# Gathers and scatters of a mixture-of-experts layer with 128 rows instead of 96

## What is computed

```python
scores = sigmoid(h @ w_router)
_, top_idx = top_k(scores + router_bias, 8)
top_w = top_s / sum(top_s) * 2.5
hmid = silu(h @ w_gate_e) * (h @ w_up_e) * gate     # each expert: 1024 -> 256
out = x + shared(h) + sum over chosen experts of hmid @ w_down_e   # 256 -> 1024
```

## Time and profile before

| | |
|---|---|
| median of 3 runs | 1163.53 us (1160.26 to 1170.39) |
| the profiled execution's own time | 1162.66 us |
| its span, first to last instruction | 1160.7 us |
| TensorE matmuls | busy 1116.2 us, 96% |
| VectorE | busy 875.0 us, 75% |
| ScalarE | busy 718.3 us, 62% |
| GpSimd | busy 337.8 us, 29% |
| DMA over the span | 284.64 MB, 245 GB/s; 16 engines |

### The profile page before, as it was taken

One profiled execution on the slowest core, in us unless ns is written; L12 is line 12 of the kernel. 1 busy time (PEld: TensorE's weight loads), 2 busy tenths in 40 slices (PEclk: granted clock), 3 DMA queues, 4 the chain that ended last, 5 costly groups with the idle time before them and its releaser, 6 DMA issues.

```text
span 1160.7 us, 18736 instructions
## 1 busy us (share of the span) xinstructions
PE 1116.2 (96%) x5682; PEld 828.7 (71%) x5682; DVE 875.0 (75%) x1445; ACT 718.3 (62%) x1218; POOL 337.8 (29%) x293
## 2 busy tenths in 40 slices
PE   7999999999999999999999999999999999999994
PEld 5889978777775575567777777777677767777772
DVE  6543385578753534589999999999899888999982
ACT  5434455453435111258888888888787877878882
POOL 0221021000000001136333344444444443455542
PEclk7999999999999999999999999999999999999997
DMA  5333221422422175459999999999999999999962
GB/s 182 129 90 117 85 72 39 152 66 82 119 82 82 64 322 203 170 209 381 370 365 366 373 370 369 368 360 368 367 368 368 354 353 356 368 364 365 363 193 32
DMA packets 65606, 284.64 MB, mean 245 GB/s; under 512 B 12515, under 2 KB 15083, under 8 KB 40604
## 3 DMA queue, kind: packets, MB, share of 16 engines
q1 hardware_dynamic: 51228, 250.50, 57.6%
q0 software_dynamic: 14336, 33.59, 12.2%
HBM read 271.40 MB, written 29.42 MB: 259 GB/s over the span
## 4 chain that ended last, share of the span: by engine, by line
DMA 47%; POOL 3%; issue 3%; POOLq 1%; DVE 0%
DMA out<-arena,idxs 47%; POOL turn L561 3%; POOLq L328 0%; POOL out L571 0%; POOLq L577 0%; POOLq L597 0%; POOLq L581 0%; DVE w_lo L1286 0%; POOLq L582 0%
## 5 line engine op out<-in xcount | busy, mean ns | idle before, releaser
L1657 PE MATMUL bank<-gu_parts,xT_parts 128*96 128x512 f32 x1280 | 343.6, 398 | 4.5 <-DVE xT_parts L1274 3.6
L1657 PEld LDWEIGHTS bank<-gu_parts,xT_parts 128*96 128x96 f32 x1280 | 202.0, 162 | 88.2 <-DVE xT_parts L1274 4.1
L561 POOL TENSOR_TENSOR turn<-minus_half 16x1 f32<-16x1 f32 x128 | 149.9, 1171 | 367.6 <-DMA out<-arena,idxs 319.4
L1672 PE MATMUL bank<-w_lo 128*96 128x512 f32 (+1 forms) x816 | 204.9, 400 | 3.9 <-issue 2.9
L1672 PEld LDWEIGHTS bank<-w_lo 128*96 128x96 f32 (+1 forms) x816 | 130.7, 167 | 51.1 <-issue 4.3
L1281 DVE TENSOR_TENSOR gu_parts<-arena_x,gu_parts 128x1024 fp32r<-128x1024 f32 x96 | 116.7, 1216 | 18.9 <-ACT gu_parts L862 18.9
L1488 PE MATMUL bank<-w_hi,hT_hi 128*128 128x512 f32 (+1 forms) x320 | 125.8, 393 | 3.7 <-DVE arena L1232 2.2
L1281 DVE TENSOR_TENSOR gu_parts<-arena,gu_parts 128x1024 fp32r<-128x1024 f32 x96 | 116.8, 1216 | 14.6 <-ACT gu_parts L862 14.6
L862 ACT ACTIVATE gu_parts<-arena_x 128x1024 fp32r<-128x1024 f32 x96 | 101.4, 1056 | 40.2 <-DMA arena_x<-in_w_up_e 28.8
L1488 PE MATMUL bank<-w_hi,hT_lo 128*128 128x512 f32 (+1 forms) x320 | 122.7, 383 | 0.0
L1488 PE MATMUL bank<-w_lo,hT_hi 128*128 128x512 f32 (+1 forms) x320 | 122.4, 383 | 0.0
(11 more groups left out here) (190 smaller groups left out, 1929.8 us busy)
## 6 DMA issues: line engine op xcount, KB each, us to landing
arena<-in_w_gate_e SPq DMA_DIRECT2D x32, 1024.0 KB
arena<-in_w_up_e SPq DMA_DIRECT2D x32, 1024.0 KB
arena<-in_w_down_e SPq DMA_DIRECT2D x32, 1024.0 KB
arena_x<-in_w_gate_e SPq DMA_DIRECT2D x32, 1024.0 KB
arena_x<-in_w_up_e SPq DMA_DIRECT2D x32, 1024.0 KB
arena_x<-in_w_down_e SPq DMA_DIRECT2D x32, 1024.0 KB
arena<-in_w_in SPq DMA_DIRECT2D x14, 1024.0 KB, 5.4
arena<-in_w_gate SPq DMA_DIRECT2D x8, 1024.0 KB, 5.8
```

The source lines that it names most:

```text
L561: nc.gpsimd.tensor_tensor(turn[:], minus_half[0:16, 0:1], minus_half[0:16, 0:1], ALU.add).then_inc(turns, 1)
L1657: last = nc.tensor.matmul(out_, a[:, PER * c + j, :], b[c][:, :, j, :], start=(c == 0 and j == 0 and i == 0), stop=(c == CHUNKS - 1 and j ...
L1672: last = nc.tensor.matmul(psY[h][0:rows, :], midT[n][a][:, j, 0:rows], w[b][:, j, h * 512:(h + 1) * 512], start=(j == 0 and k == 0), stop= ...
```

## The change

Both kinds of transfer take all 128 rows. `iota_b` is filled for 16 runs of eight partitions, slot m * 16 + i in partition 8 i + m, and `held` cuts the first six of each eight out of a tile: only these columns of the one-hot tile are ever written, the others stay zero from one memset, and their index is out of bounds. There are 96 slots as before. The weights of TensorE for the gathered rows, for `mid` and for the slots have 128 columns in place of 96, and the outputs 128 rows; the copies on ScalarE and VectorE of transposed data handle the same 96 columns as before in 16 runs of six, those that work by rows handle 128 partitions.

```diff
-        xT_hi, xT_lo = (xT_parts[:, k * ND * SLOTS:(k + 1) * ND * SLOTS].rearrange("p (j s) -> p j s", j=ND) for k in range(2))
+        xT_hi, xT_lo = (xT_parts[:, k * ND * P:(k + 1) * ND * P].rearrange("p (j s) -> p j s", j=ND) for k in range(2))
...
+        def held(t):
+            return t.rearrange("p j (i m) -> p j i m", i=DMA_ENGINES)[:, :, :, 0:SLOTS // DMA_ENGINES]
...
         def turned_rows(c):
-            return psT[c][:].rearrange("p (j s) -> p j s", j=HALF)[:, :, 0:SLOTS]
+            return psT[c][:].rearrange("p (j s) -> p j s", j=HALF)
+        def these_rows(k):
+            return (lambda t: t) if isinstance(k, int) and k == 0 else held
...
-                pool.indirect_dma_start(out=xg[slot][0:SLOTS, :], out_offset=None, in_=hn_dram,
-                                        in_offset=bass.IndirectOffsetOnAxis(idxg[slot][0:SLOTS, 0:1], 0),
+                pool.indirect_dma_start(out=xg[slot], out_offset=None, in_=hn_dram,
+                                        in_offset=bass.IndirectOffsetOnAxis(idxg[slot][:, 0:1], 0),
...
-                pool.indirect_dma_start(out=out_rows, out_offset=bass.IndirectOffsetOnAxis(idx[0:SLOTS, 0:1], 0),
-                                        in_=y[slot][0:SLOTS, :], in_offset=None, bounds_check=last_row, oob_is_err=False,
+                pool.indirect_dma_start(out=out_rows, out_offset=bass.IndirectOffsetOnAxis(idx[:, 0:1], 0),
+                                        in_=y[slot], in_offset=None, bounds_check=last_row, oob_is_err=False,
...
-                    nc.scalar.activation(xT_hi[:, c * HALF:(c + 1) * HALF, :], turned_rows(c), ACT.Copy).then_inc(xT_hi_ready, 1)
+                    nc.scalar.activation(these_rows(k)(xT_hi[:, c * HALF:(c + 1) * HALF, :]), these_rows(k)(turned_rows(c)), ACT.Copy).then_inc(xT_hi_ready, 1)
...
+            for n in range(2):
+                nc.vector.memset(onehot[n], 0.0)
...
-                return nc.vector.tensor_tensor(onehot[n][:, :, 0:SLOTS], iota_b[:, 0:SLOTS].unsqueeze(1).broadcast_to([P, NT, SLOTS]),
-                                               col.broadcast_to([P, NT, SLOTS]), ALU.is_equal)
+                to = held(onehot[n])
+                return nc.vector.tensor_tensor(to, held(iota_b[:].unsqueeze(1)).broadcast_to(to.shape), col.unsqueeze(3).broadcast_to(to.shape), ALU.is_equal)
...
-                    last = nc.tensor.matmul(psI[0:SLOTS, 0:6], onehot[n][:, t, 0:SLOTS], table[:, t, bass.ds(e, 1), :].rearrange("p a b -> p (a b)"),
+                    last = nc.tensor.matmul(psI[:, 0:6], onehot[n][:, t, :], table[:, t, bass.ds(e, 1), :].rearrange("p a b -> p (a b)"),
...
-                    last = nc.tensor.transpose(psT[j // HALF][:, c:c + SLOTS], xg[slot][0:SLOTS, j::ND], ident[0:SLOTS, 0:SLOTS])
+                    last = nc.tensor.transpose(psT[j // HALF][:, c:c + P], xg[slot][:, j::ND], ident)
...
-                    down(n, h, P if is_shared(it) else SLOTS).then_inc(y_psum, 1)
+                    down(n, h, P).then_inc(y_psum, 1)
...
-    c[:, P:P + SLOTS] = np.arange(SLOTS).reshape(SLOTS // DMA_ENGINES, DMA_ENGINES).T.reshape(-1)[None]
+    c[:, P:2 * P] = np.arange(P).reshape(P // DMA_ENGINES, DMA_ENGINES).T.reshape(-1)[None]
```

More of the change, by code:

```diff
@@ L820, in _, with silu_of, silu_i @@
             nc.scalar.activation(scoresT, psI[0:E, :], ACT.Sigmoid).then_inc(scores_sig, 1)
-            def silu_of(n, rows):
-                return nc.scalar.activation(silu[n][0:rows, :], psG[n][0:rows, 0:F], ACT.Silu)
+            def silu_of(n):
+                return nc.scalar.activation(silu[n], psG[n][:, 0:F], ACT.Silu)
             def copy_midT(n, rows):
-                return nc.scalar.activation(midT[n][0][:, :, 0:rows], psM[:, 0:NF * P].rearrange("p (j s) -> p j s", j=NF)[:, :, 0:rows], ACT.Copy)
+                these = held if rows == SLOTS else (lambda t: t)
+                return nc.scalar.activation(these(midT[n][0]), these(psM[:, 0:NF * P].rearrange("p (j s) -> p j s", j=NF)), ACT.Copy)
             def copy_y(n, h):
-                return nc.scalar.activation(y[n][0:SLOTS, h * 512:(h + 1) * 512], psY[h][0:SLOTS, :], ACT.Copy)
-            def silu_i(it, n, rows):
+                return nc.scalar.activation(y[n][:, h * 512:(h + 1) * 512], psY[h][:], ACT.Copy)
+            def silu_i(it, n):
                 act.wait_ge(gu_psum, it + 1)
                 after(act, mid_ready, it - 1)
-                silu_of(n, rows).then_inc(silu_ready, 1)
+                silu_of(n).then_inc(silu_ready, 1)
             def y_i(it, n):
@@ L905, in _ @@
                 gu_hi_k(1, 1, c)
-            silu_i(SH, 0, SLOTS)
+            silu_i(SH, 0)
             xT_hi_k(1)
@@ L1273, in xT_k @@
                     half = slice(c * HALF, (c + 1) * HALF)
-                    nc.vector.tensor_tensor(xT_lo[:, half, :], turned_rows(c), xT_hi[:, half, :].bitcast(f32), ALU.subtract).then_inc(xT_split, 1)
+                    nc.vector.tensor_tensor(these_rows(k)(xT_lo[:, half, :]), these_rows(k)(turned_rows(c)), these_rows(k)(xT_hi[:, half, :].bitcast(f32)), ALU.subtract).then_inc(xT_split, 1)
             def gu_lo_k(k, slot, c):
@@ L1283, in low_midT @@
             def low_midT(n, rows_):
-                src = psM[:, 0:NF * P].rearrange("p (j s) -> p j s", j=NF)[:, :, 0:rows_]
-                return nc.vector.tensor_tensor(midT[n][1][:, :, 0:rows_], src, midT[n][0][:, :, 0:rows_].bitcast(f32), ALU.subtract)
+                these = held if rows_ == SLOTS else (lambda t: t)
+                src = psM[:, 0:NF * P].rearrange("p (j s) -> p j s", j=NF)
+                return nc.vector.tensor_tensor(these(midT[n][1]), these(src), these(midT[n][0].bitcast(f32)), ALU.subtract)
             def low_wd(slot, h):
@@ L1709, in midT_i @@
                 after(pe, midT_ready, it)
-                transpose_mid(n, P if is_shared(it) else SLOTS).then_inc(midT_psum, 1)
+                transpose_mid(n, P).then_inc(midT_psum, 1)
             def find_i(it, n):
@@ L1785, in _ @@
                         pe.wait_ge(w_in_sem[0][k], 4 * E + 16 * it + 16)
-                    gate_up(0, SLOTS, xT_all, 0).then_inc(o_gu, 1)
+                    gate_up(0, P, xT_all, 0).then_inc(o_gu, 1)
                     pe.wait_ge(o_mid, it + 1)
-                    transpose_mid(0, SLOTS).then_inc(o_midT_psum, 1)
+                    transpose_mid(0, P).then_inc(o_midT_psum, 1)
                     pe.wait_ge(o_midT, it + 1)
                     pe.wait_ge(o_wd, it + 1)
-                    down(0, 0, SLOTS)
-                    down(0, 1, SLOTS).then_inc(o_y_psum, 1)
+                    down(0, 0, P)
+                    down(0, 1, P).then_inc(o_y_psum, 1)
                     pe.wait_ge(o_y, it + 1)
```

20 lines of the change are left out of this document (10 added, 10 removed).

## The result

The changed kernel takes 1227.24 us (median; 1225.65 to 1229.6), the kernel before beside it 1161.89 us: a ratio of 1.0551, 95% interval 1.0511 to 1.0590. That is 65.35 us slower. The direction was forecast, the size was three times too small, and the result lies 5 us above the range.

What follows compares the result with a forecast made beforehand. TensorE was taken to bound the early experts, weight loading the late ones, with the scatter chain equally long. Chain growth of +15.6 us early and +5.4 late gave +21 on the profiled 1162.66: 1184 us, range 1142 to 1222.

Steps and rivals of the forecast that it cites:

- The scatter chain: Experts: each scatter into `out` waits for the last to land; 9.60 us apart early, 10.37 late, as long as the period.
- The signs given for it: Experts: 18432 packets, same bytes, landing near 9.4 us, one regime about 10.3 us, scatter waits up, up-weight waits down.
- the rival of the half of the engines: Indirect transfers: half the engines get eight rows with data, the others almost none; about 1253 us, chance 0.18.
- the term for the scatter's landing: Scatter: empty rows 0.63 us and POOL's work 0.17, together 0.8 us for each scatter, between 0 and 1.1.
- eight rows for each engine, the same four with data, four empty: Indirect transfers of 128 rows: how rows were taken to fall on each engine, bytes unchanged, 144 packets.
- The 0.63 itself: Scatter: two more empty rows, each with a weight packet of 0.315 us, put the completion up to 0.63 us later.
- 0.65 and 0.15: Expert period: growth in us for each of the first 24 periods (+15.6 us) and the last 36 (+5.4 us).
- the aligned partitions give back nothing: Gather beside weight loads: less conflict was worth 0.5 to 0.7 us an expert, at most 24.5 us in all; taken as 0.
- the rival (0.6 us an expert in the late stretch, 1142 us): Gather and weights: the conflict goes and the chain has slack, late period 9.7 us; 1142 us, chance 0.18.
- The two ends that I let cancel: Aligned partitions: at most 24.5 us gained, at least below nothing as the same writes meet on fewer partitions; taken as 0.
- the wider instructions: TensorE, VectorE and ScalarE at 128 wide: under 0.1 us an expert on TensorE, set at nothing.
- POOL's own 0.17 us: POOL's work for each scatter of 128 rows: 0.17 us more, a third of the upper end 0.48.

Runs made afterwards that it cites:

- e1_quads: The changed kernel with slots laid out for a deal in fours, three of each four partitions in use; 1138.78 us.
- e5_scatter_96: The changed kernel with slots in sixes over the first 96 partitions, the gather kept at 128 rows, the scatter back at 96; 1142.56 us.
- e7_ports_worst: e2_96_wide with only the slot order inside each engine's six partitions changed, so rows crowd on fewer groups of four partitions; 1174.52 us.
- the square: Four kernels, slots in sixes, gather/scatter rows: 96/96 1162.8 us, 128/96 1142.56, 96/128 1188.44, 128/128 1193.78.
- e2_96_wide: The changed kernel with both transfers back at 96 rows filled by sixes, all other instructions still 128 wide; 1162.8 us.
- e3_112: e2_96_wide with transfers of 112 rows, seven partitions for each engine, six of them in use; 1154.0 us.

## Why the prediction was wrong

**Right: what bounds the kernel, and by which mechanism it would slow.** The scatter chain was named as long as the expert period and as what becomes the bound when it grows. The signs given for it came in kind: 18432 packets and unchanged bytes, ScalarE waiting for scatters (3.3 us before, 170.7 after), the up-weight waits nearly gone, one regime instead of two. Their sizes did not: the landing was to be 9.4 us before 750 us and was about 10.4, the period about 10.3 and was 11.15. The rate stayed under 340 GB/s all through (333 and 325), which was the sign named for the rival of the half of the engines.

**Wrong: the term for the scatter's landing.** The step that failed is "eight rows for each engine, the same four with data, four empty". The bytes were right and the deal was not: the fullest engine has 7.92 rows with data on average instead of 4.47. I priced two empty rows at 0.63 us beside a weight packet each. The time from a scatter's issue to the turn that it releases in fact grew by 1.7 us in the first stretch (8.8 to 10.4) and by 1.1 in the second (9.3 to 10.4). `e1_quads`, with the same 32 empty rows more, has 9.0 and 9.3 us there; so all but a few tenths are the deal. The rows with data alone grew by 2.2 us in their span (2.55 to 4.79, first stretch); from the last of them to the released turn it is then 0.8 us in place of 1.6, which gives some back, and why is not shown.

The 0.63 itself rested on a wrong reading of the earlier trace rows. Of the 24 packets under 512 B only 15 are of POOL's queue; the other 9 are of the weight queue, and 60 beside 71 does not tell whether a weight packet goes between two empty rows. After the change 64 empty rows pass in 0.24 us (807.72 to 807.96). By the deal in fours they are eight for each engine that has no data, and a weight packet before each would have made it 8 x 0.309 = 2.5 us.

The period of the experts became, by the scatters' spacing, 11.15 us: 1.55 more than 9.60 in the first stretch and 0.78 more than 10.37 in the second. With the forecast's 24 and 36 periods that is 37 + 28 = 65 us, as measured; with the SiLU's 9.62 and 10.30 us in their place it would be 67, so the agreement to the microsecond is chance. The forecast had 0.65 and 0.15.

**Wrong: the aligned partitions give back nothing.** The conflict did go, 432 GB/s against 317, and the price put on it in the rival (0.6 us an expert in the late stretch, 1142 us) is nearly what `e5_scatter_96` and `e1_quads` got, 1142.56 and 1138.78; their late period is 9.8 us by the SiLU (757.8 to 1080 us), where the rival had 9.7. The two ends that I let cancel did not: the thought that rows on fewer partitions would meet more weight writes did not hold for gathers of 128 rows, wherever their rows lay: in the six kernels that have them 5 to 7% of the weight packets took over 340 ns (527 to 1080 us), in the five whose gathers have 96 or 112 rows 18 to 26%. The reading that fits is that in a transfer of 128 rows the engine that writes a row is the one that loads the weights there; the traces do not name the engine of a packet, so it is argued and not shown. In the 96-row form crowding does cost: 11.7 us in `e7_ports_worst`. The statement that the gain would lie under the longer chain in any case was right for the changed kernel, and the square shows it: 20 us of gain under the short scatter, none under the long one.

**Right: the wider instructions.** Taken as nothing; 0.9998 (0.9971 to 1.0024) in `e2_96_wide`. POOL's own 0.17 us measured 0.147.

**The rivals.** "The rows with data fall on half of the engines" was the case, at a chance of 0.18 and 1253 us. Its price was too high, and its parts were wrong: it charged gathered and scattered rows alike, 2.2 us an expert, less 0.7. By the square the gather's extra rows are hidden beside the scatter chain; and it left out that a weight packet goes behind each row. 3.45 rows more at 0.327 + 0.309 us are 2.2, the growth of the scattered rows' span. Its own sum was not consistent either: 11.8 against a mean period of 10.0 is 1.8 and not 1.5, and 60 times that is 108 us.
The Trainium skill (DMA: Bandwidth & Descriptors, The descriptor swizzle) gives the deal of a plain transfer to 128 partitions: four and four, 32 apart. The runs agree, for transfers by index too: this rule is what `e1_quads` was built on, and it was 88 us faster than the deal in eights that the filling assumed. I gave it 0.18 because no row of before showed a 128-row transfer by index; a rule about the same number of partitions from the same queue deserved more than that.
The Trainium skill (SBUF — State Buffer, Door 1: The DMA port swizzle) has fours of partitions on ports, two fours that are 32 apart on each. `e7_ports_worst` was laid out by that rule and took 11.7 us more than `e2_96_wide`, so it agrees in direction; the size at one port was not measured.

**What stays open.** `e1_quads` is 3.8 us faster than `e5_scatter_96`, with the same 4.47 rows; the intervals of their ratios overlap, and if it is real, the aligned scatter, the even gather, or both can be the cause. And how much of `e3_112`'s gain is place and how much is the empty row's timing.

## What to carry to other kernels

Before laying out rows for "one engine each", find out how this very transfer is dealt: at 96 rows the kernel's sixes fitted, at 128 rows the same idea with eights put all the load on half of the engines. The sign in a profile is a DMA share that falls below its full value (0.91 for 1.02) while something waits for a DMA: engines as a group are free, and some of them are not. Two edits that come in one change are to be priced and tried apart; with the slots in sixes the gather's half was worth -20 us and the scatter's +51, and laid out for the true deal both together give 1138.78 us, 2% below the kernel before.

## What was not expected of the hardware

- A row index out of bounds costs little: 32 more of them for each transfer, and POOL's issue is 0.147 us longer, the scatter's landing 9.0 us in `e1_quads` against 8.9 in `e2_96_wide` (where gathers still disturb). In the changed kernel 64 of them passed in 0.24 us.
- Gathered rows of a 96-row transfer and the weights beside them slow each other. In means over half a microsecond a gathered row took up to 214 ns before and 159 after, a weight packet beside it up to 437 and 309. By queue, the gather's stretch of before (690.8 to 692.8 us), to be read against the one of after shown above:

```profile
q1 hardware_dynamic: 64, 0.46, 75.0%
q0 software_dynamic: 59, 0.18, 27.7%
```

- With the conflict gone the same engines move more at the same busy share: 383 GB/s at 1.02 in `e1_quads`, 369 at 1.02 in `e2_96_wide`, 361 at 1.03 in `e7_ports_worst`. A full DMA share says that engines are occupied, not that they move what they could.
